# Expert 0 of a routed layer: its context rows picked by a one-hot product before the latent lists, and its latent row factor picked on chip

## The reference

```python
h2 = rmsnorm(x, norm2_g) * (1 + sc2) + sh2            # shift and scale differ for latent and context tokens
aff = softmax(h @ w_router)                           # over 16 experts
gate, idx = top_k(aff.T, cap)                         # cap = 64 latent tokens, 16 context tokens per expert
xs = h[idx]
hid = silu(xs @ w_gate) * (xs @ w_up)                 # 2048 -> 1024
out = (hid @ w_down) * gate                           # 1024 -> 2048
x = x + g2 * scatter_add(out, idx)
```

## Time and profile before

| | us |
|---|---|
| median of 3 runs | 2101.21 (2101.08 to 2101.26) |
| span of the profiled execution | 2099.3 |
| TensorE busy | 2027.9 (97%) |
| VectorE busy | 1139.3 (54%) |
| ScalarE busy | 478.1 (23%) |
| GpSimd busy | 165.3 (8%) |
| DMA, mean over the span | 292 GB/s |

### The profile page before, as it was taken

One profiled execution on the slowest core, in us unless ns is written; L12 is line 12 of the kernel. 1 busy time (PEld: TensorE's weight loads), 2 busy tenths in 40 slices (PEclk: granted clock), 3 DMA queues, 4 the chain that ended last, 5 costly groups with the idle time before them and its releaser, 6 DMA issues. The chain is left out here.

```text
span 2099.3 us, 37670 instructions
## 1 busy us (share of the span) xinstructions
PE 2027.9 (97%) x15045; PEld 1128.7 (54%) x15045; DVE 1139.3 (54%) x2673; ACT 478.1 (23%) x846; POOL 165.3 (8%) x236
## 2 busy tenths in 40 slices
PE   6999999999999999999979999999999999999995
PEld 3578878888878887888842333333333333333331
DVE  4369988997558877777255243343233333223314
ACT  4232222222257776222210000000000000000003
POOL 1020010111000001112110000000000000000001
PEclk9999999999999999999989999999999999999998
DMA  9956667563120006665489999999999999999997
GB/s 389 409 188 219 213 231 257 202 221 112 69 103 1 2 1 236 227 201 187 158 308 378 406 413 417 416 416 421 424 416 416 417 416 415 429 416 416 417 395 318
DMA packets 71924, 614.03 MB, mean 292 GB/s; under 512 B 8432, under 2 KB 10104, under 8 KB 29104
## 3 DMA queue, kind: packets, MB, share of 16 engines
q1 hardware_dynamic: 47392, 514.36, 59.3%
q0 software_dynamic: 18672, 84.89, 13.3%
q10 hardware_dynamic: 5776, 13.63, 1.9%
HBM read 583.28 MB, written 29.60 MB: 292 GB/s over the span
## 5 line engine op out<-in xcount | busy, mean ns | idle before, releaser
L1261 PE MATMUL ps<-arena 128*32 128x512 f32 x6144 | 662.6, 592 | 0.6 <-DVE arena L2315 0.6
L1261 PEld LDWEIGHTS ps<-arena 128*32 128x32 f32 x6144 | 199.4, 110 | 458.6 <-issue 457.7
L1288 PE MATMUL ps<-arena 128*32 128x512 f32 x3072 | 332.8, 592 | 2.6 <-DVE arena L2326 1.8
L702 PE MATMUL ps<-B_w_hi,B_x_hi 128*128 128x512 f32 x720 | 286.7, 398 | 6.0 <-DVE B_x_lo L2098 3.3
L704 PE MATMUL ps<-B_w_lo,B_x_hi 128*128 128x512 f32 x720 | 281.5, 391 | 0.0
L703 PE MATMUL ps<-B_w_hi,B_x_lo 128*128 128x512 f32 x720 | 281.3, 391 | 0.0
L1288 PEld LDWEIGHTS ps<-arena 128*32 128x32 f32 x3072 | 99.6, 110 | 232.9 <-issue 228.6
L2347 DVE COPY arena<-arena 128x16 f32 x1200 | 156.6, 182 | 98.6 <-issue 98.6
L2323 DVE TENSOR_TENSOR arena<-ps,arena 64x256 f32<-64x256 f32 x96 | 39.9, 416 | 297.9 <-ACT arena L1618 297.3
L1618 ACT ACTIVATE arena<-ps 64x512 f32<-64x512 f32 x48 | 28.5, 594 | 609.0 <-PE ps L1261 609.0
L702 PEld LDWEIGHTS ps<-B_w_hi,B_x_hi 128*128 128x128 f32 x720 | 135.5, 188 | 45.6 <-issue 12.6
(11 more groups left out here) (286 smaller groups left out, 2027.4 us busy)
## 6 DMA issues: line engine op xcount, KB each, us to landing
arena<-in_w_expert SPq DMA_DIRECT2D x192, 2048.0 KB, 12.8
arena<-in_w_in_b SPq DMA_DIRECT2D x36, 1024.0 KB, 5.0
arena<-in_w_mod_q SPq DMA_DIRECT2D x32, 1024.0 KB, 19.2
arena<-in_w_mod POOLq DMA_DIRECT2D x32, 1024.0 KB, 5.7
arena<-in_w_mod POOLq DMA_DIRECT2D x32, 512.0 KB, 4.3
arena<-in_w_out_b SPq DMA_DIRECT2D x16, 1024.0 KB, 6.4
arena<-in_w_mod POOLq DMA_DIRECT2D x64, 256.0 KB, 3.3
arena<-in_x_sample SPq DMA_DIRECT2D x8, 1024.0 KB, 10.2
```

Source lines behind the costliest of these rows:

```text
L702: eng.matmul(out, x_hi, w_hi, start=start, stop=False)
L1261: mm = pe.matmul(bank(g)[32 * q:32 * q + 32, :], e_rows, w[q], start=start, stop=stop, skip_group_check=True)
L1288: mm = pe.matmul(bank(b)[32 * q:32 * q + 32, :], hT[g][:, f, :], w_four[q], start=f == 0, stop=f == 7, skip_group_check=True)
```

## The change

Context first. After the second top-k round DVE copies the 16 context places and gives a signal; PE spreads expert 0's row of them over all partitions; DVE compares it with the token number `tok_id` and multiplies by the norm factor, which gives `picked`, a 128 x 16 matrix with one entry per column. PE multiplies the context rows by it, 16 products that pick and turn at once. The first 1536 columns of these rows come back from `x1_d` by a load (786 KB) on SP's queue ahead of units 2 to 5, as `ctx_rows`; the last 512 are in SBUF. ACT writes `xC` from PSUM, with scale and shift, in 16 activations. Pair 0 of the context products of expert 0 is done before the latent lists are turned, and pairs 1 to 4 behind them, ahead of the gathered rows.

Latent rows: the gather takes 64 rows without padding. Their norm factor is picked on DVE (`r_picked`) and spread on a diagonal (`spread`, an activation), and a product of the raw gathered rows with it both turns and scales.

```diff
@@ SP
                 after_out(sp, 2 * c + 1)
+                if c == 15:
+                    sp.wait_ge(early_stored, 96)
+                    sp.dma_start(ctx_rows, x1_d[LAT:TOK, 0:3 * NB]).then_inc(ctx_in, 16)
@@ PE, behind the turn of the logits
-            pe.wait_ge(out_taken, 4 * NT)
+            for _ in range(10):
+                pe.matmul(bank(4)[:, 0:P], ident[:, :], ident[:, :], ...)
@@ PE, behind the turn of the norm factors
             pe.wait_ge(route_ready, 3)
+            pe.matmul(bank(5)[:, 0:CX], ctx[:, 0:1].broadcast_to([4 * NE, P]), idxf[:, 0:CX], ...).then_inc(route_turned, 1)
...
+            for _ in range(6):
+                pe.matmul(bank(0)[:, 0:P], ident[:, :], ident[:, :], ...)
+            pe.wait_ge(ctx_in, 16)
             pe.wait_ge(route_ready, 4)
-            pe.wait_ge(flip_ready, 1)
-            pe.matmul(bank(4)[0:CL, 0:2 * NE], flip, ...).then_inc(route_turned, 1)
-            for _ in range(22):
-                pe.matmul(bank(0)[:, 0:P], ident[:, :], ident[:, :], ...)
-            pe.wait_ge(cols_ready, 2)
-            pe.wait_ge(cols_ready, 3)
-            pe.matmul(bank(7)[0:NE, 3 * P:3 * P + CAP], off_of[:, :], ...).then_inc(route_turned, 1)
+            for k in range(KC):
+                cols = left[:, k // 2, k % 2, :] if k < 12 else right[:, (k - 12) // 2, k % 2, :]
+                mm = pe.matmul(ctx_turned(k), cols, picked, ...)
+                if k in (3, KC - 1):
+                    mm.then_inc(t1_done, 1)
+            def latent_lists():       # the turns of the latent lists and the flip, moved here
+            def column_places():      # the turn of the places table, moved here
@@ gathered_transposes
-                    pe.wait_ge(xs_scaled, g + 1)
+                    pe.wait_ge(gathered, 16)
+                    pe.wait_ge(spread_ready, 1)
+                    pe.wait_ge(cols_ready, 3)
                     for k in range(k0, k0 + n):
-                        mm = pe.transpose(..., xsP[0:CAP, P * k:P * (k + 1)], ident[0:CAP, 0:CAP])
+                        mm = pe.matmul(..., xs_cols[:, k // 2, k % 2, :], spread[0:CL, :], ...)
@@ expert(e, first)
-                    latent_pair(e, i, (0, 1))
-                    context_pair(i)
+                    last = latent_pair(e, i, (0, 1))
+                    if not first or i >= CTX_AHEAD:
+                        last = context_pair(i)
+                    last.then_inc(xused, 2)
                     if first and i < 2:
                         gathered_transposes((2 + i,))
+                    if first and i == 2:
+                        column_places()
...
-            pe.wait_ge(route_ready, 5)
+            for i in range(LISTS_AFTER):              # LISTS_AFTER, CTX_AHEAD = 1, 5
+                context_ahead(i)
+            latent_lists()
+            for i in range(LISTS_AFTER, CTX_AHEAD):
+                context_ahead(i)
             gathered_transposes((0, 1))
@@ ACT
-            act.wait_ge(gathered, 16)
-            for k0, n, _ in FIRST:
-                act.activation(xsP..., by_pairs(xs...), ACT.Copy, scale=xs[0:CAP, D:D + 1]).then_inc(xs_scaled, 1)
+            for k in range(KC):
+                ...
+                act.activation(xC[:, k, 0:CX], ctx_turned(k), ACT.Identity, bias=..., scale=...).then_inc(xC_ready, 1)
             act.wait_ge(cols_ready, 2)
+            act.activation(spread[0:CL, :], ident[0:CL, 0:CL], ACT.Copy, scale=r_picked[:, 0:1]).then_inc(spread_ready, 1)
@@ POOL
-            pool.wait_ge(ms2_ready, 2)
-            for t in range(NT):
-                pool.dma_start(x1_d[P * t:P * (t + 1), D:D + ROW_PAD], rstdP[:, t, :]).then_inc(r_stored, 16)
+            pool.iota(tok_row, [[1, LAT]], ...).then_inc(flip_ready, 1)
-            pool.indirect_dma_start(xs[0:CAP, :], None, x1_d[:, :], ... idxC[:, 0:1] ...)
+            pool.indirect_dma_start(xs[0:CL, :], None, x1_d[:, :], ... idxC[0:CL, 0:1] ...)
@@ DVE, top-k rounds
+                if r == CX // 8 - 1:
+                    dve.tensor_copy(idxf[:, 0:CX], idx[:, 0:CX]).then_inc(route_ready, 1)
+                if r == CX // 8:
+                    dve.wait_ge(route_turned, 3)
+                    dve.tensor_scalar(picked, bank(5)[:, 0:CX], tok_id[:, 0:1], rstd2[:, TL:TL + 1], ALU.is_equal, ALU.mult)\
+                        .then_inc(route_ready, 1)
@@ DVE, behind the latent lists
+            link(dve.scalar_tensor_tensor(out=tok_row, in0=tok_row, scalar=later[0:CL, 0:1], in1=bank(6)[0:CL, 0:LAT], ...))
+            dve.tensor_reduce(r_picked[:, :], tok_row, AX, ALU.add).then_inc(cols_ready, 1)
-            (the places table: 2291 to 2299)
@@ DVE, behind the four groups of FIRST and ahead of 2389
+            (the places table, with wait_ge(route_turned, 7) ahead of its copy)
```

More of the change, by code:

```diff
@@ L413, in build @@
         oT_hi, oT_lo = [parts_D["oT_hi"][i] for i in HI_AT], parts_D["oT_lo"]
-        xs = at(H0, D + ROW_PAD)
-        xsP = at(W0 + 4096, D)
+        xs = at(H0, D)
+        tok_row = at(W0 + 4608, LAT)[0:CL, :]
+        spread = at(W0 + 4096, CL)
+        picked = at(W0 + 4096 + CL, CX)
         xstage = at(H0 + 2064, KC, CAP)
@@ L461, in build @@
         rstd2 = sb("rstd2", [P, NT])
-        rstdP = sb("rstdP", [P, NT, ROW_PAD])
+        r_picked = sb("r_picked", [CL, 1])
         cst2 = sb("cst2", [2, 2 * NE])
@@ L1220, in _ @@
             pe.wait_ge(route_ready, 3)
+            pe.matmul(bank(5)[:, 0:CX], ctx[:, 0:1].broadcast_to([4 * NE, P]), idxf[:, 0:CX], start=True, stop=True,
+                      skip_group_check=True).then_inc(route_turned, 1)
             for n, what in ((0, idxf), (1, vals)):
-                for half, rows in ((1, high), (0, low)):
-                    mm = pe.matmul(bank(3)[0:CL, NE * (2 * half + n):NE * (2 * half + n + 1)], what, rows, start=True, stop=True,
-                                   skip_group_check=True)
@@ L1234, in _ @@
[L1234 to L1239 removed]
+                pe.matmul(bank(7)[CL:CAP, 4 * P - 2 * NE + NE * n:4 * P - 2 * NE + NE * (n + 1)], what[:, 0:CX], ctx, start=True,
+                          stop=True, skip_group_check=True)
@@ new lines, in latent_lists @@
+            def latent_lists():
+                pe.wait_ge(route_ready, 5)
+                for n, what in ((0, idxf), (1, vals)):
+                    for half, rows in ((1, high), (0, low)):
+                        mm = pe.matmul(bank(3)[0:CL, NE * (2 * half + n):NE * (2 * half + n + 1)], what, rows, start=True,
+                                       stop=True, skip_group_check=True)
+                mm.then_inc(route_turned, 1)
+                pe.wait_ge(route_ready, 6)
+                pe.wait_ge(flip_ready, 1)
+                pe.matmul(bank(4)[0:CL, 0:2 * NE], flip, slots[:, 1].rearrange("p n e -> p (n e)"), start=True, stop=True,
+                          skip_group_check=True).then_inc(route_turned, 1)
@@ L2380, in _ @@
                     link(ins)
-                ins = shifted(slice(k0, k0 + n))
+                ins = shifted_latents(slice(k0, k0 + n))
                 if g != 2:
                     ins.then_inc(xsT_ready, 1)
+            dve.wait_ge(cols_ready, 3)
+            dve.wait_ge(out_done, 4 * NT)
+            link(dve.tensor_copy(row_of[:, :], idxC[:, 0:NE]))
+            link(dve.tensor_scalar(tile_of[:, :], row_of[:, :], float(P), None, ALU.is_ge))
+            for t in range(2, NT):
+                link(dve.scalar_tensor_tensor(out=tile_of[:, :], in0=row_of[:, :], scalar=float(P * t), in1=tile_of[:, :],
+                                              op0=ALU.is_ge, op1=ALU.add))
+            dve.scalar_tensor_tensor(out=off_of[:, :], in0=tile_of[:, :], scalar=float(D - P), in1=row_of[:, :],
+                                     op0=ALU.mult, op1=ALU.add).then_inc(cols_ready, 1)
+            dve.wait_ge(route_turned, 7)
+            dve.tensor_copy(offs[:, :], bank(7)[0:NE, 3 * P:3 * P + CAP]).then_inc(route_ready, 1)
             dve.wait_ge(x_placed, NT)
```

120 lines of the change are left out of this document (66 added, 54 removed).

## The result

Six runs of the changed kernel have a median of 2108.94 us (2106.75 to 2110.01), six of the kernel before 2101.17 us. The ratio is 1.0031, 95% interval 1.0021 to 1.0040: slower by 6.5 us (4.4 to 8.4). I had forecast 2104.3 us, no measurable change, in a range that ended at 2107.3. The profiled execution of the changed kernel took 2109.91 us with a span of 2108.1, so the two spans to be compared differ by 8.8 us, 2.3 us more than the medians.

The account below looks back on a forecast made before the run. DVE's chain was taken to set when expert 0's down products begin, with fixed PE work behind. Span 2099.3 + 0.6 + 0.0 + 2.5 = 2102.4 us; time 2101.2 + 3.1 = 2104.3 us, range 2100.8 to 2107.3.

Parts of the forecast that it names:

- What bounds the kernel: DVE sets when expert 0's down products begin, 31.76 us after its in-place products; from there PE's work is fixed.
- (a): Turn of the logits to latent list: dummies +0.4 and DVE additions +0.4 us, no delay from pair 0; list at 1075.4.
- (b): Gather, from latent list to rows in use: 6.1 us, bounds 5.8 and 8, with `fgB` meeting only its last rows.
- (c): Four context pairs behind the lists: end at 1082.6, later than the gather, so PE sets the start.
- (d): From there to the first latent product: 1.4 us, product at 1084.0, +0.6 us, bounds -0.5 and +2.5.
- (e): First latent product to DVE's in-place products: three latent pairs, turns and places table, 12.8 us, change 0.0.
- the spared work buys nothing: PE's first half: the 8.6 us of context work spared there only lengthens PE's wait, 9.6 us instead of 1.8.
- (f): Expert 0's down products: clock falls to 0.50 in PE's 9.6 us wait and returns late, costing 2.5 us.
- rival 1: Seam runs late through low clock or late lists: first latent product +2.5, clock loss 3.6, time 2107.3; chance 0.25.
- Rival 3: Spared PE work counts because DVE's chain gets shorter: end at 2093 if fully won; chance 0.07 for over 4.2 us.
- rival 4: `picked` or the context load comes late, so context pair 0 holds the lists up several us: 2110; chance 0.03.

Follow-up runs that it names:

- e4: Changed kernel with expert 0's hidden values on DVE behind 48 of the 80 column copies instead of all 80; 0.9984 of the kernel before.
- e8: Kernel before with expert 0's hidden values on DVE behind 64 of the 80 column copies instead of all 80; 0.9990 of the kernel before.
- e10: Kernel before with the `fgB` load issued when the lists are ready, beside the gather instead of behind it; 1.0009 of the kernel before.
- e2: Changed kernel with no context pair ahead of the latent lists and all five behind; 1.0033 of the kernel before.
- e3: Changed kernel without its ten dummy products ahead of the turn of the affinities; 1.0040 of the kernel before.
- e9: Changed kernel with late `fgB`, hidden values behind 40 column copies, and all five context pairs behind the latent lists; 0.9970 of the kernel before.
- e12: Changed kernel with late `fgB`, hidden values behind 40 column copies, and no ten dummies ahead of the affinities' turn; 0.9966 of the kernel before.
- e5: Changed kernel with 30 dummy products in PE's wait ahead of expert 0's down products; 1.0026 of the kernel before.
- e6: Changed kernel with only context pair 0 ahead of the latent rows, pairs 1 to 4 behind their latent pairs; 1.0060 of the kernel before.
- e11: Changed kernel with 40 dummy products in PE's wait ahead of expert 0's down products; 1.0012 of the kernel before.
- e1: Changed kernel with the `fgB` load, and `G2` behind it, issued only when the gathered rows have landed; 1.0017 of the kernel before.
- e7: Changed kernel with `fgB` behind the gather and hidden values behind 40 of the 80 column copies; 2094.23 us, 0.9964 of the kernel before.

## Why the prediction was wrong, point by point

- **What bounds the kernel:** right. The stretch from the in-place products to the down products is 31.76 and 31.77 us, and e4 shows that it is DVE's order. Behind that PE has one wait left, for weights near the end, of 0.5 us in the changed kernel's profile and 0.7 in the earlier trace rows. So what moves the first down product moves the end.
- **(a) the latent lists, +0.8:** too small in the profiled run, +3.15. The ten dummies ran wholly at half clock (4.61 us, my upper end), +2.0 where I took +0.4. Pair 0 took 3.55 us, also at half clock, and held the lists up 1.5 us, for which I took nothing. The turn of the lists itself was 0.5 us shorter, at full clock. DVE's additions cost 0.3, less than the 0.4. In the ten profiles of experiments with the changed seam (all but e8 and e10) the list stands at 18.8 to 21.8, on average 20.2, so my +0.8 (20.7) is near the middle of them, and the changed kernel's own profile, 23.1, is the latest. How much the list is late in its other five executions isn't known. No edit of the seam's order (e2, e3, e9, e12) gave a time that can be told apart.
- **(b) the gather, 6.1 us:** the step that failed. I took 6.1 us with an upper bound of 8. From the list to the turn of the rows it took 8.8 us here and 8.8 to 9.0 us wherever `fgB` went out beside it and PE was free (e3, e4, e5, e6, e11), against 6.8 in e1 and 6.4 in e12, the two with the loads behind it. I saw that `fgB` would be issued some 2 us after the list, and reckoned that it meets only the last rows. But POOL issues the gather itself 1.0 us after the list, and its data start a microsecond or more after that the earlier trace rows. The two are issued 0.44 us apart and move together until `fgB` has landed. The loads of `G2`, which I hadn't thought of, follow before the rows have landed. The 0.5 us that I took off for 64 rows instead of 80 doesn't show either: with nothing beside them 64 rows took 5.3 to 5.7 us from issue to landing and 80 rows 5.4 and 5.6. In the runs this is worth 2.9 us (e1 against the changed kernel, 0.2 to 5.7) and, for `fgB` alone, 1.9 (e10 against before, 0.0 to 3.6). With this step put right, in e1, the kernel's ratio is 1.0017, which is 2104.8 us, against my 2104.3. That this is so close is partly luck, since smaller errors offset each other there: in e1's profile the first latent product comes 0.2 us earlier than before (forecast +0.6), the way to the in-place products takes 1.0 us more (forecast 0.0), and the down products take 2.8 us more (forecast 2.5).
- **(c) and (d), the pairs and the first latent product:** which of pairs and gather ends last depends on the clock. I had the pairs last (1082.6); they ended at 1083.4, but the gather was later. The turn took 1.55 us, 1.4 forecast.
- **(e) the way to the in-place products, 0.0:** partly wrong, +2.69. The structure was right, three latent pairs and then the table. The 20 passes of the turns took 2.6 us (1.55 and 1.08 until the pairs resume), where I had 1.8; 13.73 us is the whole with a full clock (e1, e4, e7, e12; 13.74 in e2), +1.0. The other 1.7 us are a low clock in the first pair (5.34 us for 32 passes instead of 3.64), behind the wait for the gather; it is there in each trace in which PE waits 2.7 to 2.9 us for the rows (the changed kernel, e3, e5, e11), and in none of those in which it waits 1.65 us or less. That "the spared work buys nothing" was too strong, as e6 shows.
- **(f) the clock behind the wait, +2.5:** right, +2.46 in the trace, and e11 removes it with nothing else changed.
- **The rivals:** the time, 2108.9, came out beyond rival 1 (2107.3). Its place was right, a seam that runs late: the first latent product stood at +4.3 us in the profile, where rival 1 has +2.5. But it named only the clock and the late lists, and not the gather against `fgB`. Rival 3, the spared work does count, is false for this change. With DVE's order changed it looks true: the reordered kernels are 7.6 us (e7) and 2.1 us (e8) faster than before, the one with the spared work and the other without. Of rival 4 there is no trace: PE never waits for the context load.

What stays open: how much of the slower median comes from the late list, what `G2` costs the gather by itself, and how much of the spread of 2106.5 to 2111.5 us in the runs of e3 comes from where in the seam the clock is low. One profile for each kernel can't tell.

## What to carry to other kernels

Before filling an idle hole of one engine, look for the wait behind it. Here PE already waited 1.8 us for another engine's queue, in which 80 copies stood ahead of the values that were wanted. So most of the 8.6 us of work moved ahead turned into a longer wait, with low clock behind it. The same change with that queue reordered and the late loads is 7.6 us faster than before. When a wait is taken out of an engine's queue, list every load behind it: that load now starts earlier and may stand beside the transfer on the path.

## What the runs showed of the hardware

- A gather of 64 rows of 8 KB took 7.7 us from issue to landing with a load of 1 MB issued 0.44 us behind it and 0.65 MB more some 4 us behind it, and 5.7 us (e1) without them. A gather of 80 rows took 6.7 us with the 1 MB load 0.75 us ahead of it (e10) and 5.4 us without.
- 9.2 us of useless products in a wait of 9.6 us shortened the work behind it from 23.25 to 20.81 us. A rest of the wait of 2.22 us (e4) or 2.75 us (e5) was still followed by 22.5 us, with a clock that was 1.00 in the wait and fell to 0.50 only when PE was at work again. A wait of 1.83 us in the earlier trace rows was followed by 20.81.
- The same code before the affinities' turn, ten products of 20 passes, took 2.48 us in e5 (granted clock 1.00) and 4.61 us in the changed kernel (0.50). Seam times of one profile have some 2 us of this in them, which is as much as the edits in question.
